# Two-block transformer kernel on one core: expert products in four 32-column groups, slot sums in three banks

## The reference, cut to what matters

```
logits = h @ router_w + router_b          # 256 tokens, 8 experts
top_p, top_i = top_k(softmax(logits), 2)  # two experts for each token
for e in range(8):
    out += combine[..., e:e+1] * ((silu(h @ w1[e]) * (h @ w3[e])) @ w2[e])
```

## Time and profile before

| what | value |
|---|---|
| median of three runs | 2436.21 us |
| the profiled execution: its time | 2435.68 us |
| its span (first to last instruction) | 2433.9 us |
| TensorE busy | 2338.6 us, 96% of the span |
| expert stage, first L892 to last L915 | 739.3 us |

### The profile page before, as it was taken

One profiled execution on the slowest core, in us unless ns is written; L12 is line 12 of the kernel. 1 busy time (PEld: TensorE's weight loads), 2 busy tenths in 40 slices (PEclk: granted clock), 3 DMA queues, 4 the chain that ended last, 5 costly groups with the idle time before them and its releaser, 6 DMA issues.

```text
span 2433.9 us, 48425 instructions
## 1 busy us (share of the span) xinstructions
PE 2338.6 (96%) x21484; PEld 1846.0 (76%) x21484; DVE 872.5 (36%) x1839; ACT 475.3 (20%) x871; POOL 26.5 (1%) x62
## 2 busy tenths in 40 slices
PE   7999899999999989979999999999999999999998
PEld 6888777777687867677777777777767877888884
DVE  3666553655433655221110110110112442352453
ACT  2342321000125333110000000000002431232332
POOL 2000000000000000000000000000000000000000
PEclk9999999999999989979999999999998999999999
DMA  9553165777433213539999999999981323333220
GB/s 360 205 190 121 70 219 196 267 278 279 161 139 139 104 55 119 194 139 388 381 386 391 377 395 393 377 393 394 393 326 72 121 87 138 137 123 122 104 87 18
DMA packets 75526, 537.97 MB, mean 221 GB/s; under 512 B 8552, under 2 KB 8560, under 8 KB 11440
## 3 DMA queue, kind: packets, MB, share of 16 engines
q1 hardware_dynamic: 72864, 526.14, 56.5%
q0 software_dynamic: 1360, 4.85, 0.6%
q10 hardware_dynamic: 1088, 3.81, 0.4%
HBM read 529.90 MB, written 4.85 MB: 220 GB/s over the span
## 4 chain that ended last, share of the span: by engine, by line
PE 89%; DVE 5%; ACT 4%; issue 1%; POOL 1%; DVEq 0%; ACTq 0%; POOLq 0%
PE ps L892 20%; PE ps L426 16%; PE ps L456 16%; PE ps L911 6%; PE ps L437 6%; PE ps L915 4%; PE ps L726 3%; PE ps L846 3%; PE ps L498 2%; PE ps L751 2%; PE ps L1061 2%; ACT ring L1393 1%; DVE ring L1782 1%; PE ps L1015 1%; PE ps L640 1%
## 5 line engine op out<-in xcount | busy, mean ns | idle before, releaser
L892 PEld LDWEIGHTS ps<-hT,ring 128*64 128x64 f32 x11264 | 472.3, 138 | 42.8 <-issue 38.4
L892 PE MATMUL ps<-hT,ring 128*64 128x96 f32 x11264 | 489.2, 248 | 8.3 <-DVEq L2415 4.2
L426 PE MATMUL ps<-ring,hT 128*128 128x256 f32 x2176 | 482.8, 382 | 6.0 <-ACT RA L1393 6.0
L426 PEld LDWEIGHTS ps<-ring,hT 128*128 128x128 f32 x2176 | 413.9, 192 | 64.4 <-issue 8.6
L456 PE MATMUL ps<-ring,hT 128*128 128x256 f32 x1792 | 403.9, 382 | 1.8 <-DVE hT L1773 1.3
L456 PEld LDWEIGHTS ps<-ring,hT 128*128 128x128 f32 x1792 | 337.6, 191 | 52.4 <-issue 4.2
L1773 DVE TENSOR_TENSOR RA<-ps,RA 128x192 f32<-128x192 f32 (+1 forms) x99 | 39.1, 395 | 700.6 <-PE ps L892 615.1
L1393 ACT ACTIVATE RA<-ps 128x192 f32<-128x192 f32 (+2 forms) x159 | 69.9, 440 | 1122.2 <-PE ps L892 609.3
L911 PE MATMUL ps<-ring,RA 128*64 128x512 f32 x704 | 167.6, 595 | 0.0
L437 PE MATMUL ps<-hT,ring 128*128 128x256 f32 (+1 forms) x768 | 155.3, 363 | 0.1
L437 PEld LDWEIGHTS ps<-hT,ring 128*128 128x128 f32 x768 | 135.9, 190 | 19.3 <-issue 2.4
(11 more groups left out here) (294 smaller groups left out, 1797.0 us busy)
## 6 DMA issues: line engine op xcount, KB each, us to landing
ring<-stream SPq DMA_DIRECT2D x497, 1024.0 KB, 6.7
slots_scratch<-YT ACTq DMA_DIRECT2D x7, 384.0 KB, 7.3
x_rows<-x SPq DMA_DIRECT2D x2, 512.0 KB, 8.3
gates_row<-bgate SPq DMA_DIRECT2D x1, 1024.0 KB, 11.4
QT<-bgate SPq DMA_DIRECT2D x1, 1024.0 KB, 14.2
rows_scratch<-RB ACTq DMA_DIRECT2D x2, 512.0 KB, 4.5
out<-x_rows SPq DMA_DIRECT2D x2, 512.0 KB, 2.6
rowt<-rows SPq DMA_DIRECT2D x1, 460.0 KB, 9.5
```

What stands on the lines that cost most here:

```text
L426: m = pe.matmul(ps[:, b, t * UC:(t + 1) * UC], lhs[:, k, t * P:(t + 1) * P], ring[:, s, k * UC:(k + 1) * UC], start=k == 0, stop=k == KC - 1)
L892: m = pe.matmul(ps[64 * j:64 * (j + 1), b, c * CAP:(c + 1) * CAP], ring[:, s, k * UC + c * P + 64 * j:k * UC + c * P + 64 * (j + 1)], hT[: ...
```

## The change

The weights of a w1 or w3 unit are split in four groups of 32 columns in place of two groups of 64. The slots of a w2 product are split in three groups of 32, which go to banks 4, 5 and 6, and the 1024 output columns in four of 256, so that all products of an expert use four column groups of 32. VectorE takes the sums as twelve operations of 32 x 256. The semaphore counts follow, and `back_to_tokens` uses banks 2 and 3 in place of 6 and 7.

```diff
--- before.py
+++ after.py
@@ -29,11 +29,12 @@
 EXPERT_UNITS = 3 * FG
 CAP = 96
 ZERO_ROW = (NE - 1) * CAP
-WIDE = 64
+SLOT_TILE = 32
+SLOT_BANKS = (4, 5, 6)
 PASSES = (2, 3)
 SLOT_BASE = [0] + [ZERO_ROW + 1 + i * NE * CAP for i in range(len(PASSES))]
 SLOT_ROWS = [ZERO_ROW + 1, ZERO_ROW + 1 + len(PASSES) * NE * CAP]
-INCS = {"w1m": 2, "w3m": 2, "w2m": 4}
+INCS = {"w1m": 4, "w3m": 4, "w2m": 4}
 EXPERT_INCS = FG * sum(INCS.values())
 EPS = 1e-6
 NEG = -1e30
@@ -297,7 +298,7 @@
 
 
         gain = {unit_done: EXPERT_INCS, burst_for_dve: 3,
-                act_took: FG, dve_took: FG + 4, dve_gave_pe: 1, dve_step: 20,
+                act_took: FG, dve_took: FG + 4, dve_gave_pe: 1, dve_step: 26,
                 dve_gave_act: 1}
         full = {}
         MAIN = [("m", e) for e in range(NE)]
@@ -825,7 +826,7 @@
                 for n in range(2):
                     pe.wait_ge(*from_dve.more())
                     for t in range(T):
-                        b = (6, 0)[t] + n
+                        b = (2, 0)[t] + n
                         free(b)
                         m = pe.matmul(ps[:, b, :], back[0:CAP, t, :], slot_rows[0:CAP, n * 512:(n + 1) * 512],
                                       start=True, stop=True)
@@ -888,9 +889,9 @@
                 b = next_bank("U")
                 for c in range(2):
                     for k in range(KC):
-                        for j in range(2):
-                            m = pe.matmul(ps[64 * j:64 * (j + 1), b, c * CAP:(c + 1) * CAP],
-                                          ring[:, s, k * UC + c * P + 64 * j:k * UC + c * P + 64 * (j + 1)],
+                        for j in range(4):
+                            m = pe.matmul(ps[32 * j:32 * (j + 1), b, c * CAP:(c + 1) * CAP],
+                                          ring[:, s, k * UC + c * P + 32 * j:k * UC + c * P + 32 * (j + 1)],
                                           hT[:, k, 0:CAP], start=k == 0, stop=k == KC - 1)
                             if c and k == KC - 1:
                                 m.then_inc(unit_done, 1)
@@ -903,20 +904,18 @@
                 s = landed_unit(turn)
                 need(("w3", l, g))
                 if g == 0:
-                    free(4)
-                    free(5)
-                flags = [dict(start=g == 0 and k == 0, stop=g == FG - 1 and k == 1) for k in range(2)]
+                    for b in SLOT_BANKS:
+                        free(b)
                 for k in range(2):
-                    for j in range(2):
-                        pe.matmul(ps[64 * j:64 * (j + 1), 4, :], actT_e[:, g % 2, k, 0:WIDE],
-                                  ring[:, s, k * D + 512 * j:k * D + 512 * (j + 1)], **flags[k])
-                for k in range(2):
-                    for j in range(4):
-                        m = pe.matmul(ps[32 * j:32 * (j + 1), 5, 0:256], actT_e[:, g % 2, k, WIDE:CAP],
-                                      ring[:, s, k * D + 256 * j:k * D + 256 * (j + 1)], **flags[k])
-                        if k:
-                            m.then_inc(unit_done, 1)
-                            done.more()
+                    for i, b in enumerate(SLOT_BANKS):
+                        for j in range(4):
+                            m = pe.matmul(ps[32 * j:32 * (j + 1), b, 0:256],
+                                          actT_e[:, g % 2, k, i * SLOT_TILE:(i + 1) * SLOT_TILE],
+                                          ring[:, s, k * D + 256 * j:k * D + 256 * (j + 1)],
+                                          start=g == 0 and k == 0, stop=g == FG - 1 and k == 1)
+                            if k and b == SLOT_BANKS[-1]:
+                                m.then_inc(unit_done, 1)
+                                done.more()
                 full["y", l, 1] = (4, unit_done, done.n)
 
             def expert(l, turn=None, next_at=None):
@@ -931,7 +930,7 @@
                     if g >= 1:
                         expert_down(l, g - 1, turn)
                 expert_down(l, FG - 1, turn)
-                taken_by("dve", [4, 5], ("y", l, 0))
+                taken_by("dve", SLOT_BANKS, ("y", l, 0))
                 if next_at:
                     need(("pick", l, 1))
 
@@ -2276,13 +2275,12 @@
 
             def slot_rows_out():
 
-                for j in range(2):
-                    stt(slot_rows[0:WIDE, 512 * j:512 * (j + 1)], ps[64 * j:64 * (j + 1), 4, :], slot_w[0:WIDE, 0:1],
-                        gates_l[1][0:WIDE, 1, 512 * j:512 * (j + 1)], ALU.mult, ALU.mult)
                 for j in range(4):
-                    stt(slot_rows[WIDE:CAP, 256 * j:256 * (j + 1)], ps[32 * j:32 * (j + 1), 5, 0:256],
-                        slot_w[WIDE:CAP, 0:1], gates_l[1][WIDE:CAP, 1, 256 * j:256 * (j + 1)], ALU.mult, ALU.mult,
-                        c=took if j == 3 else step)
+                    for i, b in enumerate(SLOT_BANKS):
+                        lo, hi = i * SLOT_TILE, (i + 1) * SLOT_TILE
+                        stt(slot_rows[lo:hi, 256 * j:256 * (j + 1)], ps[32 * j:32 * (j + 1), b, 0:256],
+                            slot_w[lo:hi, 0:1], gates_l[1][lo:hi, 1, 256 * j:256 * (j + 1)], ALU.mult, ALU.mult,
+                            c=took if j == 3 and b == SLOT_BANKS[-1] else step)
                     if j in (1, 3):
                         yield j
```

## The result

Four runs of the changed kernel give a median of 2707.24 us (2704.51 to 2710.52), beside 2435.89 us for the kernel before in four runs: a ratio of 1.1113, 95% interval 1.1094 to 1.1133. The change makes the kernel 11% slower. The profiled execution has a span of 2708.8 us, 274.9 more than before. Lines moved by one: L892 is now L893, and L912 stands for both L911 and L915.

The account below looks back on a forecast made before the run. TensorE and the weight stream were near their limits, with instruction fetch taken to decide after the change. Fetch 253, clock 10 and slot-sum end 1.5 made 264.5 us on a 2433.9 us span: 2698, time 2700, range 2540 to 2900.

Parts of the forecast that it names:

- (e): Instruction fetch in the expert stage: 211 blocks of 256 at 4.7 us each, 992 us of stage, 253 more.
- (f): TensorE's clock in the expert stage: halts lower the granted clock, costing 10 us, with 0 and 40 as ends.
- (a): w1 and w3 products: instructions double to 256 matmuls and 256 loads a step, the array's time stays.
- (b): w2 products: 2.58 us a step instead of 2.87, changes of group width gone, saving 25.5 us over 88 steps.
- (c): Slot sums on VectorE: twelve operations make TensorE wait 14 us over seven times, plus 1.5 us after the last expert.
- The lower end: Fetch chain per block with DMA engines nearly idle (share 0.07): 3.0 us, which the array's 3.29 would cover at no cost.
- the upper end: Highest cost given for the lowered clock in the expert stage: 40 us.
- The rival by the Trainium skill's page: TensorE start limit: about 25 ns between matmul starts, 17 ns more a pass, 96 us, 2522; start limit's chance 0.05.

Follow-up runs that it names:

- e2: Kernel before with only the w1 and w3 products in four groups of 32, w2 and slot sums as before: 2698.82 us, ratio 1.1066.
- spread version: Kernel before with four groups of 32 in the first half of every w1 and w3 unit (also called spread kernel): 2552.89 us, ratio 1.0477.
- paired version: Kernel before with the w2 products of two steps made together, groups of 64 first, then of 32: 2430.58 us, ratio 0.9962.
- e1: Changed kernel with w1 and w3 back at two groups of 64, so only the w2 part and slot sums: 2461.32 us, ratio 1.0096 against the kernel before.
- thin stream: Changed kernel, but from the 12th expert unit on each stream DMA brings 128 of 2048 columns: 2521.45 us, ratio 1.0351.
- half stream: Changed kernel, but from the 12th expert unit on each stream DMA brings 1024 of 2048 columns: 2614.37 us, ratio 1.0732.
- two partial kernels: e2 (2698.82 us) and e3 (2552.16 us), each with a part of the change alone on the kernel before.
- e3: Kernel before with four groups of 32 in the w1 units alone: 2552.16 us, ratio 1.0465.
- narrow w1 units with the thin stream: Kernel before with four groups of 32 in w1 units alone and 128 of 2048 stream columns from the 12th expert unit on: 2435.84 us, ratio 0.9998.

## Why the prediction was right

It forecast 2700 us, in a range of 2540 to 2900, with 0.85 on slower; measured are 2707. The mechanism is the forecast one; that the number came so near is in part luck, since by the estimates below (e) was some 23 us too large and (f) some 31 too small.

- **(a), instructions double, the array's time stays.** Right: 22528 matmuls of L893 and 4224 of L912, and passes of 0.082 us inside a block.
- **(b), 25.5 us saved at the changes of width.** No gain shows here, as forecast: with w2 narrow too the time is 8 us above e2's. The price of 0.29 us for a pair of changes holds: the spread version's step has it to the hundredth, and in the paired version 48 pairs saved made 8 us net, some 13 with the added halts, where 14 were forecast.
- **(c), slot sums 14 + 1.5 us.** The first is right by e1's run, 12.9 us in seven waits for ScalarE; in the changed kernel 1.9 us of such waits are left, hidden as forecast. The 1.5 us after the last expert were too much: the wait before L831 is 3.4 us where L830's was 3.0.
- **(e), the fetch chain.** The mechanism is right: halts at block borders, one packet every 4.79 us for a forecast 4.7, a stage of 1009.9 us for a forecast 992, q8 packets 279 for 278. The working is less good than its result. The lower end, 3.0 us, was read beside a branch at nearly idle DMA engines, where another program state could differ; in the changed kernel with the thin stream the chain is 3.6 to 3.9 us. For the thin and the half stream the forecasts were 76 to 101 and 79 us too low.
- **(e), means instead of blocks.** A second slip: the sum took the longer of two means, the array's and the chain's. What counts is nearer to the longer of the two for each block. That would explain the two partial kernels, which took 59 and 74 us more than forecast: with narrow w1 units a block takes 4.9 us in the array on the mean, the forecast chain was 5.2, and the measured distance is 125 packets in 700 us, 5.6. A block that lies in the narrow units takes 2.64 us and halts, and the long blocks around it give nothing back. An estimate, worked out block by block over the pattern of a step (e3's: 49 instructions in 2.87 us, 257 in 2.64, 129 in 2.64), gives 115 us of halts for a chain of 5.2 us, where 113 were lost; the longer of the means gave 42. For e2 a chain of 4.8 to 5.0 us gives 225 to 249 us (260 lost), for the spread kernel 5.2 us gives 85 (91 lost). But the same rule with 3.57 us gives 18 us for the narrow w1 units with the thin stream, where the trace has 2.9. The lost times hold the clock's share too. So the rule is argued and not shown, and something of a long block's time can be kept. In the changed kernel nearly all blocks are short, so this slip mattered little there.
- **(f), the clock, 10 us.** Too small. The granted clock is 0.94 in the stage for 0.99 before. 106 us of the stage passed at the level of 1.2 GHz, and 1784 of the 26836 matmuls started in them: 16.9 a us, beside 27.7 in the rest of the stage at 2.4 GHz. An estimate from these rates is that the clock cost some 41 us, the upper end that the prediction gave. Its reason for 10 was that L893 needs 5.3 us a block at the lower level, hardly more than the chain. The stretch at 1408 shows what was missing: TensorE is busy throughout, with the DMA engines at 0.05. Over all 106 us it is busy for 95% with a DMA share of 0.33, so the stream is mostly away there, the chain is likely nearer to its 3.6 us, and the slow array is the bound. That leaves about 230 of the 271 us for (e), where 253 were forecast: at the full clock a block takes 4.6 us, and the 4.79 hold the clock's share too.

The Trainium skill, Runtime: NRT & Kernel Launch, section on instruction fetch mechanics, calls a block border mostly hidden. Here it is where a block keeps TensorE busy for more than some 6 us, and with the stream away for the narrow w1 units too (they cost some 5 us then). It is not where block after block is run in 2.6 us, even with the stream away (3.57 us from one to the next).
The rival by the Trainium skill's page TensorE: Matmul & The Clock Gate, no two matmul starts under about 25 ns, is contradicted by the trace: 20.5 ns on the mean over 128 of them.

## What to carry to other kernels

Count instructions as a resource of their own: in these kernels a stretch of TensorE code whose 256 instructions ran in less than 3.6 to 3.9 us, or in less than 4.8 to 6.2 us under a full stream of DMA, was bound by their fetch, whatever the array could do. Halts also lower the granted clock, and that is a cost of its own (some 41 us here). In a profile the fetch shows as idle "issue" before matmuls at distances of 256 instructions and as packets of the instruction queue. Splitting a product into more column groups doubles its instructions and leaves its streaming time alone; to save on changes of group width (0.29 us for a pair of them here), put products of one width next to each other.

## What was not expected of the hardware

- With the DMA engines at 0.12 it still took 3.57 us from one block to the next (1336.70 to 1340.27), where 3.0 had been read beside a branch.
- Four column groups side by side keep the pass of 0.082 us that two groups have, with eight instructions in it instead of four. Nothing in TensorE itself slowed them.
- The packet distance is 4.79 us at a DMA share of 0.76 (the changed kernel) and 5.6 at 0.88 (narrow w1 units). The second number includes blocks that the array itself needs some 6 us for (2.87 us of w2, 2.64 of w3 and the rest of w1), so the distance alone is no measure of the chain.
- A mean DMA share can hide two states: in the changed kernel it is 0.76, but 0.33 in the 106 us in which TensorE works at the lower clock.
